# The norm's sum for the second half of a recurrent head, made inside the first chunk of the next head

## What is computed

```python
def step(state, xs):
    qch, kch, vch, b = xs                       # one chunk of one head, b = running sum of log decay
    ...
    scores = jnp.einsum('bhtd,bhsd,bhtsd->bhts', qch, kch, decay)
    o = jnp.einsum('bhts,bhsv->bhtv', scores, vch)
    o = o + jnp.einsum('bhtd,bhdv->bhtv', qch * jnp.exp(b), state)
    state = jnp.exp(b_last[:, :, 0, :])[..., None] * state + \
        jnp.einsum('bhsd,bhsv->bhdv', kch * jnp.exp(b_last - b), vch)
    return state, o
...
o_h = hgrn2(q_h, f_h, i_h, lb)
o_h = rms_norm(o_h, g_head).reshape(B, S, HG_WIDTH).astype(z_h.dtype) * jax.nn.silu(z_h)
```

## Time and profile before

| | |
|---|---|
| median of 3 runs | 3848.33 us (3847.86 to 3850.99) |
| profiled execution | 3853.37 us, span 3851.6 us |
| TensorE busy | 3520.7 us, 91% of the span |
| VectorE busy | 2110.2 us, 55% |
| ScalarE busy | 1552.9 us, 40% |
| GpSimd busy | 1372.5 us, 36% |
| chain of work that ended last | TensorE 73%, VectorE 10%, issue 7%, ScalarE 5% |

### The profile page before, as it was taken

One profiled execution on the slowest core, in us unless ns is written; L12 is line 12 of the kernel. 1 busy time (PEld: TensorE's weight loads), 2 busy tenths in 40 slices (PEclk: granted clock), 3 DMA queues, 4 the chain that ended last, 5 costly groups with the idle time before them and its releaser, 6 DMA issues.

```text
span 3851.6 us, 62125 instructions
## 1 busy us (share of the span) xinstructions
PE 3520.7 (91%) x18848; PEld 2866.5 (74%) x18848; DVE 2110.2 (55%) x5638; ACT 1552.9 (40%) x3145; POOL 1372.5 (36%) x1636
## 2 busy tenths in 40 slices
PE   8999999999999999999998999979887999798878
PEld 6887887666777878877665879867775798677747
DVE  5655555666255555655766253266665332666653
ACT  5434443444245444443444242245453222454532
POOL 6544553332624554553333612122213112222131
PEclk9999999999999999999999999999998999899979
DMA  4100012110221001012111222111111421111124
GB/s 140 34 28 28 28 34 58 36 41 26 96 91 43 29 28 33 27 33 56 41 41 37 93 83 66 57 38 35 37 30 60 156 72 58 37 35 37 30 60 156
DMA packets 217956, 206.80 MB, mean 54 GB/s; under 512 B 17948, under 2 KB 185004, under 8 KB 216668
## 3 DMA queue, kind: packets, MB, share of 16 engines
q1 hardware_dynamic: 197536, 137.80, 12.8%
q0 software_dynamic: 12208, 47.03, 3.5%
q10 hardware_dynamic: 7920, 18.45, 1.5%
HBM read 148.30 MB, written 37.01 MB: 48 GB/s over the span
## 4 chain that ended last, share of the span: by engine, by line
PE 73%; DVE 10%; issue 7%; ACT 5%; DMA 2%; POOL 1%; DVEq 1%; SPq 0%; ACTq 0%; POOLq 0%
PE banks L923 24%; PE banks L1203 8%; PE banks L1088 5%; PE banks L1140 5%; PE banks L959 5%; PE banks L1314 4%; PE banks L1262 3%; PE banks L1112 3%; PE banks L1034 2%; PE banks L1044 2%; PE banks L1165 2%; PE banks L1056 1%; PE banks L1240 1%; DVE BB L1934 1%; PE banks L1241 1%
## 5 line engine op out<-in xcount | busy, mean ns | idle before, releaser
L923 PE MATMUL banks<-H,whi 128*128 128x512 f32 x3200 | 1055.3, 411 | 14.4 <-POOL wlo L614 12.6
L923 PEld LDWEIGHTS banks<-H,whi 128*128 128x128 f32 x3200 | 581.0, 191 | 188.3 <-issue 68.2
L923 PE MATMUL banks<-H,wlo 128*128 128x512 f32 x1600 | 636.5, 398 | 0.0
L613 POOL CAST whi<-raw 128x1024 fp32r<-128x1024 f32 x150 | 162.1, 1081 | 1220.6 <-PE banks L923 557.4
L1203 PE MATMUL banks<-H,whi 128*128 128x346 f32 (+1 forms) x1536 | 384.0, 333 | 9.9 <-DVEq L408 8.0
L614 POOL TENSOR_TENSOR wlo<-raw,whi 128x1024 fp32r<-128x1024 f32 x150 | 363.7, 2425 | 12.1
L923 PEld LDWEIGHTS banks<-H,wlo 128*128 128x128 f32 x1600 | 305.5, 191 | 71.2
L1963 DVE COPY_PREDICATED AT<-lvl,banks 128x64 f32<-128x64 int32 x896 | 222.0, 248 | 173.0 <-PE banks L966 134.8
L2230 DVE TENSOR_SCALAR_CACHE_REDUCE SP<-banks 128x346 f32<-128x346 f32 (+3 forms) x432 | 201.6, 513 | 197.9 <-PE banks L1241 196.5
L1203 PEld LDWEIGHTS banks<-H,whi 128*128 128x128 f32 x1536 | 275.3, 195 | 20.2 <-issue 14.0
L1538 ACT ACTIVATE SM<-SM,stt 128x256 f32<-128x256 f32 (+1 forms) x256 | 124.7, 488 | 329.1 <-DVE stt L2076 329.1
(11 more groups left out here) (286 smaller groups left out, 7216.5 us busy)
## 6 DMA issues: line engine op xcount, KB each, us to landing
raw<-in_w_in SPq DMA_DIRECT2D x148, 512.0 KB, 3.9
raw<-in_w_out SPq DMA_DIRECT2D x64, 256.0 KB, 2.7
raw<-in_w_out SPq DMA_DIRECT2D x18, 512.0 KB, 3.3
XT<-x_resident POOLq DMA_DIRECT2D x16, 512.0 KB, 3.9
x_resident<-XT POOLq DMA_DIRECT2D x16, 512.0 KB, 2.9
XB<-x_resident POOLq DMA_DIRECT2D x16, 512.0 KB, 4.7
out_x<-XB POOLq DMA_DIRECT2D x16, 512.0 KB, 5.4
x_resident<-XB POOLq DMA_DIRECT2D x16, 512.0 KB, 6.1
```

The lines of the kernel that those rows point to most:

```text
L923: last = nc.tensor.matmul(bank(half if bk is None else bk), w[:, slot, k, :], H[:, part, a:a + 512], start=k == 0 and n == 0, stop=k == DT ...
```

## The change

The second half's sum, root and gated product are moved from the end of a head into slot 0 of the next one. On TensorE the sum stands behind the diagonal product and ahead of the projection; on ScalarE the two root steps stand behind the copy of `KI`; on VectorE the gated product stands behind the first state copy. ScalarE's square stays at the end of the head. The first head has nothing to take over, so it is written out ahead of the loop (`first=True`), and the three turns of the loop hold heads 1 and 2, 3 and 4, 5 and 6. The last head still ends with its own sum, root and product. On GpSimd only the loop's turns are cut anew; `head_tile(h + 2, 0)` gives the same tile and wait as the line that it replaces.

```diff
 # TensorE
-                def head(h, par, nxt):
+                def head(h, par, nxt, first=False):
...
                         nc.tensor.matmul(psum[6][:, P:2 * P], KB[:, par, cs], QB[:, par, cs], start=True, stop=True).then_inc(g("sd_ready"), 1)
+                        if c == 0 and not first:
+                            head_sum(hh - 1, 1)
                         if nxt:
                             project(h * 4 + 4 + c // 2, (c // 2) % 2, h * 8 + 8 + c, c2)
...
                     if not nxt:
                         value_transposes()
-                    head_sum(hh, 1)
+                        head_sum(hh, 1)
...
+                head(0, 0, True, first=True)
                 with pe.Fori(0, HEADS // 2 - 1) as j:
-                    head(j * 2, 0, True)
                     head(j * 2 + 1, 1, True)
-                head(HEADS - 2, 0, True)
+                    head(j * 2 + 2, 0, True)
                 head(HEADS - 1, 1, False)
 # ScalarE
                         nc.scalar.copy(KI[:, c % 2, :, :].rearrange("p a b -> p (a b)"), psum[3][:, P:3 * P]).then_inc(g("ki_ready"), 1)
+                        if c == 0 and not first:
+                            norm_rstd(hh - 1, 1)
...
                     norm_square(hh, 1)
-                    norm_rstd(hh, 1)
+                    if not nxt:
+                        norm_rstd(hh, 1)
 # VectorE
                         if c < NSLOT - 1:
                             carry(hh, par, c)
+                        if c == 0 and not first:
+                            normed(hh - 1, h - 1, 1)
...
-                    normed(hh, h, 1)
+                    if not nxt:
+                        normed(hh, h, 1)
 # GpSimd
-                            if j == 1 and after:
+                            if j == 1:
                                 head_tile(h + 2, 0)
-                            elif j == 1:
-                                split_in(L * WP_A + e0 // 2, 0, i0 + I_HEAD - 2)
...
+                head(0, 0, True)
                 with pool.Fori(0, HEADS // 2 - 1) as j2:
                     o_h = own.enter(j2, "pool_h")
-                    head(j2 * 2, 0, True, True)
-                    head(j2 * 2 + 1, 1, True, True)
+                    head(j2 * 2 + 1, 1, True)
+                    head(j2 * 2 + 2, 0, True)
```

More of the change, by code:

```diff
@@ L661, in _, with head @@
                 e0 = 4 * HEADS
-                def head(h, par, nxt, after):
+                def head(h, par, nxt):
                     hh = L * HEADS + h
@@ L694, in _ @@
                 exponents(0, 2)
+                head(0, 0, True)
                 with pool.Fori(0, HEADS // 2 - 1) as j2:
                     o_h = own.enter(j2, "pool_h")
-                    head(j2 * 2, 0, True, True)
-                    head(j2 * 2 + 1, 1, True, True)
+                    head(j2 * 2 + 1, 1, True)
+                    head(j2 * 2 + 2, 0, True)
                     own.leave(o_h, HEADS // 2 - 1)
-                head(HEADS - 2, 0, True, False)
-                head(HEADS - 1, 1, False, False)
+                head(HEADS - 1, 1, False)
                 split_in(L * WP_A + e0 // 2 + 1, 0, i0 + I_HEAD + 2)
@@ L2013, in _ @@
                     apply(step)
+                head(0, 0, True, first=True)
                 with dve.Fori(0, HEADS // 2 - 1) as j2:
                     o_h = own.enter(j2, "dve_h")
-                    head(j2 * 2, 0, True)
                     head(j2 * 2 + 1, 1, True)
+                    head(j2 * 2 + 2, 0, True)
                     own.leave(o_h, HEADS // 2 - 1)
-                head(HEADS - 2, 0, True)
                 head(HEADS - 1, 1, False)
```

## The result

The changed kernel takes 3807.97 us (median of 4 runs, 3803.01 to 3814.04) against 3848.10 for the kernel before (4 runs). The ratio is 0.9897, with an interval of 0.9879 to 0.9914: 40 us less. Forecast were 62, to 3786, with a range of 3770 to 3816. The profiled execution took 3810.16 us, its span is 3808.4 against 3851.6.

The account below looks back on a forecast made before the run. TensorE was taken to bound the recurrent heads, stopped regularly by its wait for ScalarE's square. Terms of 26.3, 32.3 and 5.1 sum to 63.7, taken as 62.5: 3848.33 to 3786 us, range 3770 to 3816.

Parts of the forecast that it names:

- First term: Changes of head: the next head's block runs inside TensorE's wait for the square; 14 by 1.88 us, 26.3 us.
- Third term: Loop's turn: VectorE meets the branch while idle, so TensorE's waits of 2.53 and 2.6 us go; 5.1 us.
- TensorE at the turn: Loop's turn: TensorE's own branch costs nothing today, since level products start 0.96 us behind the sum with or without it.
- Rival three: Loop's turn: TensorE stalls without the sum's cover, four turns by up to 3.3 us, 13.2 back, 3799; chance 0.06.
- Second term: TensorE's low clock at changes of head and behind loop waits goes: eight by 3.4 and three by 1.7, 32.3 us.
- Rival one: Changes of head: low clock stays, perhaps caused by thin work; gain of 34.8 us only, 3813; chance 0.17.
- The rest of the kernel: Outside the heads: moved falls of the clock may change by some of their 1.7 or 3.4 us steps.
- rival four: Outside the heads: moved low clock multiplies by more than 62 us, kernel slower, say 3860; chance 0.02.
- rival two: Slot 1 of a head: VectorE becomes late with the masked copies, 12.6 us back, 3799; chance 0.08.

Follow-up runs that it names:

- before, square first: The kernel before, with ScalarE's square of the second half ahead of the table load instead of behind it; 3826.9 us, ratio 0.9947.
- the second profile: Profile from a second set of runs of the same changed kernel, nothing altered; 3810.2 us, ratio 0.9902.
- the filled array: The kernel before, with five thrown-away matmuls on TensorE ahead of the second-half sum in a layer's first seven heads; 3852.7 us, ratio 1.0017.

## Why the prediction came out as it did

The direction, the mechanism and the range held; the size was 22 us too large in the median. By the profiled execution, 11.2 us of that are TensorE's turn of the loop and 8.4 the rest of the kernel; about 3 are the difference between one execution and the median. By its own steps:

- **First term (26.3 us).** Right, a little small (14 by 2.0 is 28). An ordinary change lies 68.4 us from the next; forecast were 68.6. That is 2.0 us less than before, not 1.88. The wait left for the square was 0.2 to 0.3 us, not 0.58: the square comes 1.89 us behind L979 now and came 2.03 behind it before, and the block's last product ends later than its successor's usual start, from which I had counted.
- **Third term (5.1 us).** Right. VectorE meets the branch while it is idle, and no wait above 0.4 us for the masked copies is left.
- **TensorE at the turn.** The step that failed: "TensorE's own turn costs nothing today". The prediction read the 0.96 us from L991 to the level products at 364.06 as proof that the branch is free, though TensorE had just stood 2.3 us, and the sum itself still lay between. In "before, square first" a wait of 0.9 us and the sum cover it as well. With neither in front of the branch the turn costs 1.36 to 1.93 us, 6.1 in all, and three falls of the clock worth 5.1 behind it (6.6 us and two falls, 3.4, in the second profile). Rival three had this mechanism and 13.2 us, with a chance of 0.06; it came at 11.2, beside the main gain. Writing the loop out showed it. By the Trainium skill's rule on branches ("Runtime: NRT & Kernel Launch", section "Instruction fetch mechanics") a taken branch out of the instruction window stalls the engine. The traces agree, with 1.4 to 2.0 us on TensorE and 3.2 to 3.9 us on VectorE. That TensorE's rows agreed with its larger buffer, as the prediction has it, was the same misreading of a covered stall.
- **Second term (32.3 us).** In the heads the mechanism was right: every fall at an ordinary change of head went; with the three new ones at the turns set against them the profiles show 27.3 us less low clock in the heads. Taken with the first and third term and the stalls of 6.1 us (26.3 + 5.1 + 27.3 - 6.1 = 52.6), this is close to the 51.6 us measured there. Rival one is refuted, by the trace after and by the filled array. What was wrong is the size of the term for the kernel as a whole. It came from one execution, whose low clock was 169 us, while 37 runs of that kernel have a mean of 162. Over all runs the change took 14 us of low clock (162 to 148) and 24 us of time at full clock (mean span 3844.5 to 3806.5, so 3682 to 3658.5). At full clock that is what the other terms give (26.3 + 5.1 - 6.1 = 25.3); the clock gave 14 of 32.3.
- **The rest of the kernel.** Forecast as unmoved but for steps of 1.7 or 3.4 us; it grew by 8.4 us in the profiled execution and by 9.8 in the second profile. The low clock outside the heads was 136 us before, and 144 and 146 after; over all the profiles it lies between 130 and 147, with no edit in those stages. That is rival four's mechanism at a small size. TensorE's wait for GpSimd's weight split adds some in the first of the two: 12.6 us in the earlier trace rows's view of before, 16.4 after, 12.6 again in the second. What times these falls was not settled.
- **VectorE in slot 1 (rival two).** Refuted: the pair's product was short (0.69 us, and as short at all fourteen places), and the masked copies ended 0.95 us ahead of TensorE.

## What to carry to other kernels

When one engine waits at a boundary for a short chain on others, find the work of the next piece that needs nothing of it and put it in front of the wait; then move every step of the chain that blocks an in-order queue, or the gain is lost there. Before counting a stall or a branch as free, look at what covers it in the old order: a wait that is removed was also somebody's cover. Take the low clock seen in one profile as more than its removal will bring: here 25.6 us of it gave 14.0 in the heads with the loop, and 24 to 29 gave 19 to 23 without, since part of it lay over waits that came out afterwards.

## What the runs showed of the hardware

- A backward branch of a loop cost TensorE 1.36 to 1.99 us (twelve turns in three profiles) and VectorE 3.2 to 3.9 us, when nothing covered it. Written out, both stalls are gone.
- A loop has a second cost. Heads of 68.4 us were 0.6 us longer than the same heads written out, in the slots where VectorE was late.
- TensorE's granted clock fell from 2.4 to 1.2 GHz on or behind idle stretches of about 2.3 us at nine of fourteen changes of head (written out, 2.15 us: at seven, and at nine in a second profile), behind ones of 1.4 to 2.0 us at seven of twelve turns of the loop, behind 1.2 to 1.5 us at one of twelve; 0.9 us and less brought none at an ordinary change. With matmuls whose result is thrown away in the same wait there was none either. What decides at which of equal stretches it falls is not shown.
- The same kernel's total of low clock differed between executions, 153 to 173 us over the 37 runs of the kernel before, which took 3833.7 to 3855.1 us.
